# V units 0 to 119 of a two-block kernel: the weights stand in TensorE, 224 tokens move, and the result is transposed once

## The reference, cut to what matters

```python
def peer_ffn(xn, w_peer_q, sub_keys, expert_u, expert_v):
    ...                       # 128 experts and gates per token, expert_idx and gates
    def step(args):
        xc, ic, gc = args
        u = expert_u[ic]
        hval = jnp.einsum('cd,chkd->chk', xc, u).astype(jnp.float32)
        a = (gc * jax.nn.gelu(hval, approximate=False)).astype(xc.dtype)
        return jnp.einsum('chk,chkd->cd', a, expert_v[ic])
    ...
h = h + peer_ffn(rms_norm_2(h, norm_ffn_g[l]), ...)
return rms_norm_2(h, norm_final_g)
```

## Time and profile before

| | |
|---|---|
| median of 3 executions | 1364.8 us (1364.66 to 1365.86) |
| profiled execution | 1366.88 us, of which the trace spans 1365.1 us |
| PE busy | 1349.6 us (99% of the span) |
| PEld, DVE, ACT, POOL busy | 1169.7, 1060.6, 818.7, 161.5 us |
| U units 104 to 127 on TensorE | about 940.5 to 1003.9 us |
| V units 0 to 127 on TensorE | 1003.9 to about 1359.2 us |
| HBM traffic over the span | 200 GB/s read |

### The profile page before, as it was taken

The page is one execution under the profiler, slowest core; times in us unless marked ns, Lnnn a source line. Parts: engine busy times, 40 slices in busy tenths (PEclk is TensorE's granted clock), DMA queues, the critical chain, the costliest instruction groups (busy, mean ns, idle before and its releaser), DMA issues.

```text
span 1365.1 us, 21297 instructions
## 1 busy us (share of the span) xinstructions
PE 1349.6 (99%) x7896; PEld 1169.7 (86%) x7896; DVE 1060.6 (78%) x1965; ACT 818.7 (60%) x1568; POOL 161.5 (12%) x128
## 2 busy tenths in 40 slices
PE   8999999999999999999999999999999999999998
PEld 6998888888898888789999999999877777777776
DVE  6878676666787567679999899998887777777775
ACT  6876555555665554555556988886554444544444
POOL 3002030000000000000001100001333332333200
PEclk9999999999999999999999999999999999999999
DMA  6533466566544446655655544445889877777763
GB/s 223 185 120 116 136 221 187 189 194 189 167 159 137 141 139 228 203 169 172 214 188 189 193 157 153 157 156 184 298 285 348 291 286 267 280 291 287 274 197 100
DMA packets 77372, 275.38 MB, mean 202 GB/s; under 512 B 9845, under 2 KB 10357, under 8 KB 76886
## 3 DMA queue, kind: packets, MB, share of 16 engines
q1 hardware_dynamic: 67462, 239.52, 53.0%
q0 software_dynamic: 9808, 34.51, 6.6%
HBM read 270.94 MB, written 2.10 MB: 200 GB/s over the span
## 4 chain that ended last, share of the span: by engine, by line
PE 91%; DVE 4%; ACT 2%; issue 1%; DMA 1%; POOL 0%; SPq 0%; POOLq 0%; ACTq 0%; DVEq 0%
PE bank L2335 89%; DVE wl L624 1%; PE bank L2433 1%; DMA raw<-in_wts 1%; PE bank L2421 1%; ACT wh L1688 1%; DVE rows L1562 0%; ACT kdz L1694 0%; DVE St L814 0%; DVE x L1123 0%; DVE sgt L1121 0%; DVE t L774 0%; DVE us L1553 0%; DVE sg L768 0%; DVE St L811 0%
## 5 line engine op out<-in xcount | busy, mean ns | idle before, releaser
L624 DVE TENSOR_TENSOR wl<-raw,wh 128x1024 fp32r<-128x1024 f32 x429 | 523.0, 1226 | 178.3 <-ACT wh L1688 174.0
L1688 ACT ACTIVATE wh<-raw 128x1024 fp32r<-128x1024 f32 x429 | 449.1, 1055 | 240.8 <-PE bank L2335 232.4
L2335 PE MATMUL bank<-hTb,wh 128*128 128x224 f32 (+4 forms) x2208 | 560.8, 332 | 1.8 <-DVE wl L624 1.8
L2335 PE MATMUL bank<-wh,hTb 128*128 128x512 f32 (+1 forms) x1496 | 431.1, 395 | 2.2 <-DVE hTb L658 1.5
L2335 PE MATMUL bank<-hTb,wl 128*128 128x224 f32 (+2 forms) x1640 | 426.7, 274 | 0.0
L2335 PEld LDWEIGHTS bank<-hTb,wh 128*128 128x128 f32 (+1 forms) x2208 | 372.2, 190 | 26.7 <-ACT ga L2217 1.8
L2335 PEld LDWEIGHTS bank<-wh,hTb 128*128 128x128 f32 (+1 forms) x1496 | 267.5, 180 | 78.3 <-DVE hTb L1605 2.5
L2335 PEld LDWEIGHTS bank<-hTb,wl 128*128 128x128 f32 (+1 forms) x1640 | 312.1, 190 | 6.1
L2335 PE MATMUL bank<-wl,hTb 128*128 128x512 f32 (+1 forms) x748 | 247.6, 392 | 0.0
L2335 PEld LDWEIGHTS bank<-wl,hTb 128*128 128x128 f32 (+1 forms) x748 | 134.4, 180 | 36.2
L601 POOL DMA_INDIRECT rows<-in_u_rows,expert x32 | 55.9, 1745 | 299.0 <-DVE dots L1562 295.3
(11 more groups left out here) (410 smaller groups left out, 1382.9 us busy)
## 6 DMA issues: line engine op xcount, KB each, us to landing
raw<-in_wts SPq DMA_DIRECT2D x441, 512.0 KB, 3.5
x<-in_x SPq DMA_DIRECT2D x4, 256.0 KB, 7.4
sk<-in_sk SPq DMA_DIRECT2D x1, 1024.0 KB, 7.1
spill<-x SPq DMA_DIRECT2D x1, 1024.0 KB, 7.4
x<-spill SPq DMA_DIRECT2D x1, 1024.0 KB, 6.4
gb<-in_g_ffn SPq DMA_DIRECT2D x1, 512.0 KB
gb<-in_norm_mix_g SPq DMA_DIRECT2D x1, 512.0 KB
gb<-in_norm_ffn_g SPq DMA_DIRECT2D x1, 512.0 KB, 4.2
```

The source lines that it names most:

```text
L624: e.tensor_tensor(b[:, :], raw[u % RAW][:, :], a[:, :].bitcast(F), ALU.subtract).then_inc(S("lo"), 1)
L1688: e.activation(parts_of(u)[0][:, :], raw[u % RAW][:, :], ACT.Copy).then_inc(S("hi"), 1)
L2335: return e.matmul(o, l, r, start=first, stop=last, skip_group_check=True)
```

## The change

V units 0 to 119 (`DENSE = NE - 8`) are computed as the U units are: pieces of 128 columns of V rows stand in the array, and the tokens move, 448 columns (high and low) with `wh` and 224 with `wl`, 16 matmuls a unit (`part_V`). Piece k sums up over all 120 units in its own bank (`BANK_OF`), so all eight banks are in use. Units 120 to 127 are computed as before, into banks 0 to 3.

- At the start banks 2 to 5 still hold the last U units, so units 0 and 1 first go over the pieces in banks 0, 1, 6 and 7, then TensorE waits for the last U sum and goes over the other four. The last two U units' sums move from the V loop to where those of the others are.
- At the end of the 120 units the last four (`HOLD = 4`) go over the pieces in banks 0 to 3 (`FIRST`), then over those in 6, 7, 4 and 5 (`SECOND`). While the second half runs, ACT copies the low halves of the first four banks out (`lows_out`) and DVE adds the high halves (`evacuated`), and then unit 120 starts in these banks. The same follows for `SECOND` at n = 120.
- The eight sums have columns of V rows on partitions. After unit 121 TensorE turns them with 16 transposes into banks 4 to 7, and DVE adds these to `x` at n = 123 and 124 (`add_turned`).
- In the V loops `high_of` and `low_of` now come ahead of `high` and `low`. The additions of the gathered tokens (`folded`) come two units earlier, and TensorE waits before the last column range until bank 4 is free.

```diff
@@ -24,6 +24,8 @@
 SUMMED = NP + 1
 GATED = NP + 1 + NC
 SLOTS = 32
+HOLD = 4
+DENSE = NE - 8
 ORDER = list(range(NE - NP, NE)) + list(range(NE - NP - 1, -1, -1))
 K4 = (0, 1, 2, 3)
 SC = float(192) ** -0.5
@@ -127,8 +129,8 @@
         mhalf = sb("mhalf", [128, 16])
         warm = sb("warm", [128, 1])
         X0 = at[0]
-        ah = [sb(f"ah{i}", [128, 256], FR) for i in range(2)]
-        al = [sb(f"al{i}", [128, 256], FR) for i in range(2)]
+        ab = [sb(f"ab{i}", [128, 2, 256], FR) for i in range(2)]
+        ah, al = [t[:, 0, :] for t in ab], [t[:, 1, :] for t in ab]
         ge = [sb(f"ge{i}", [128, 256]) for i in range(2)]
         R0 = at[0]
         RE = nc.sbuf_usable_end // 32 * 32
@@ -390,6 +392,14 @@
                 return ah[n][:, 0:TN], al[n][:, 0:TN]
             return hTh[:, (n - 2) % 8, 0:TN], hTl[:, (n - 2) % 8, 0:TN]
 
+        def both_of(n):
+
+            return ab[n][:, :, 0:TN] if n < 2 else hTb[:, :, (n - 2) % 8, 0:TN]
+
+        def sums_of(k):
+
+            return gates[:, ORDER[k], :]
+
         def rows_of(q):
 
             return (128, TN - 128)[q]
...
+
+        BANK_OF = (0, 1, 6, 7, 2, 3, 4, 5)
+        FIRST, SECOND = (0, 1, 4, 5), (2, 3, 6, 7)
 
         ENDS = (slice(0, 512), slice(512, 768), slice(768, 1024))
         CUT = 448
@@ -1605,30 +1618,54 @@
                 e.tensor_tensor(b, gates[:, ORDER[n], :], a.bitcast(F), ALU.subtract).then_inc(S("al"), 1)
 
             at_u, at_v = slots_taken()
-            for n in range(GATED, NE - 2):
-                summed(n)
-                low(nth("U", ORDER[n]) + 2)
+            for n in range(GATED, NE):
+                if n < NE - 1:
+                    summed(n)
+                    low(nth("U", ORDER[n]) + 2)
+                else:
+                    low(nth("U", ORDER[n]) + 2)
+                    summed(n)
                 gated(n)
                 if n in (NE - 6, NE - 5):
                     low_of(n - NE + 6)
                 if n in at_u:
                     slot_taken(at_u.index(n))
+
+            def evacuated(ks, n):
+
+                for k in ks:
+                    e.wait_ge(S("u_out"), nth_sum("U", NE + n))
+                    e.tensor_tensor(sums_of(k), B[BANK_OF[k]][:, 0:TN], sums_of(k), ALU.add).then_inc(S("u_sum"), 1)
+                    n += 1
+
+            def add_turned(q):
+
+                e.wait_ge(S("in_end"), 48)
+                e.wait_ge(S("half"), 9 + q)
+                for n in range(2):
+                    xs = x[0:rows_of(q), q, two(512, n)]
+                    e.tensor_tensor(xs, B[4 + 2 * q + n][0:rows_of(q), :], xs, ALU.add).then_inc(S("used"), 1)
+
             for n in range(NE):
-                low(nth("D", "peer_expert_v_2", ORDER[n]) + LOOK)
                 if n + 2 < NE:
                     low_of(n + 2)
-                if n in (1, 2):
-                    summed(NE - 3 + n)
-                    gated(NE - 3 + n)
+                if n == DENSE - HOLD + 1:
+                    evacuated(FIRST, 0)
+                low(nth("D", "peer_expert_v_2", ORDER[n]) + LOOK)
                 if n in at_v:
                     slot_taken(at_v[n])
-                elif n - 6 in (max(at_v), max(at_v) + 1, max(at_v) + 2):
-                    folded(n - 6 - max(at_v))
+                elif n - 4 in (max(at_v), max(at_v) + 1, max(at_v) + 2):
+                    folded(n - 4 - max(at_v))
+                if n == DENSE:
+                    evacuated(SECOND, 4)
+                elif n in (DENSE + 3, DENSE + 4):
+                    add_turned(n - DENSE - 3)
             e.wait_ge(S("in_end"), 48)
+            e.wait_ge(S("used"), used_by(2 * SLOTS + 7))
 
             def add_end(n):
 
-                e.wait_ge(S("half"), 9 + n)
+                e.wait_ge(S("half"), 12 + n)
                 c, b = ENDS[n], end_of(ENDS[n])
                 if n == 1:
 
@@ -1638,11 +1675,11 @@
 
             def weighted_end(n):
                 c = ENDS[n]
-                e.wait_ge(S("used"), used_by(2 * SLOTS + 3))
+                e.wait_ge(S("used"), used_by(2 * SLOTS + 7))
                 e.wait_ge(S("x"), 19 + n)
                 e.tensor_tensor(h6[:, 1, c], x[:, 1, c], gb6[:, c], ALU.mult).then_inc(S("xg"), 1)
 
-            add_x(len(units) - 1, 8, 0)
+            add_x(len(units) - 1, 11, 0)
 
             def weighted(n):
                 c = two(512, n)
@@ -2296,21 +2333,30 @@
                     e.wait_ge(S("done"), nth("D", "peer_expert_v_2", ORDER[n - 8]) + 1)
                 copy(of_expert(n)[0], gates[:, ORDER[n], :]).then_inc(S("ah"), 1)
 
-            for n in range(GATED, NE - 2):
+            for n in range(GATED, NE):
                 block_out(n)
                 gelu(n)
                 if n in (NE - 6, NE - 5):
                     high_of(n - NE + 6)
+
+            def lows_out(ks):
+
+                for k in ks:
+                    copy(sums_of(k), B[BANK_OF[k]][:, TN:2 * TN]).then_inc(S("u_out"), 1)
+
             for n in range(NE):
-                high(nth("D", "peer_expert_v_2", ORDER[n]) + LOOK)
                 if n + 2 < NE:
                     high_of(n + 2)
-                if n in (1, 2):
-                    block_out(NE - 3 + n)
-                    gelu(NE - 3 + n)
+                if n == DENSE - HOLD + 1:
+                    e.wait_ge(S("half"), 8)
+                    lows_out(FIRST)
+                high(nth("D", "peer_expert_v_2", ORDER[n]) + LOOK)
                 if n == after_dots:
                     e.wait_ge(S("used"), used_by(SLOTS - 1))
                     e.activation(factor[:, :], dots[:, :], ACT.Gelu).then_inc(S("used"), 1)
+                if n == DENSE:
+                    e.wait_ge(S("done"), nth("D", "peer_expert_v_2", ORDER[DENSE - 1]) + 1)
+                    lows_out(SECOND)
             half_squares(5, 0, sq6)
 
             def scaled(q, c, made):
@@ -3082,13 +3128,49 @@
                 p.then_inc(S("G_ps"), 1)
             for n in range(GATED, NE):
                 early(n)
-            for n in range(NE - LAST):
-                if n == 0:
-                    e.wait_ge(S("G"), NC)
-                    e.wait_ge(S("gelu"), NE - 2)
+            def expert_of(n):
+
                 e.wait_ge(S("al"), FFT + n + 1)
-                unit_D(("D", "peer_expert_v_2", ORDER[n]), *of_expert(n), 0, n == 0, False,
+                return begin(("D", "peer_expert_v_2", ORDER[n]))
+
+            def part_V(held, n, ks):
+
+                both = both_of(n)
+                for k in ks:
+                    c, b = two(128, k), B[BANK_OF[k]]
+                    mm(b[:, 0:2 * TN], held[0][:, c], both, n == 0, False)
+                    t = mm(b[:, 0:TN], held[1][:, c], both[:, 0, :], False, n == DENSE - 1)
+                return t
+
+            e.wait_ge(S("G"), NC)
+            held = []
+            for n in range(2):
+                held.append(expert_of(n))
+                part_V(held[n], n, (0, 1, 2, 3))
+            e.wait_ge(S("u_sum"), nth_sum("U", NE - 1))
+            for n in range(2):
+                part_V(held[n], n, (4, 5, 6, 7)).then_inc(S("done"), 1)
+            for n in range(2, DENSE - HOLD):
+                part_V(expert_of(n), n, range(8)).then_inc(S("done"), 1)
+            held = []
+            for n in range(DENSE - HOLD, DENSE):
+                held.append(expert_of(n))
+                t = part_V(held[-1], n, FIRST)
+            t.then_inc(S("half"), 1)
+            for n in range(DENSE - HOLD, DENSE):
+                part_V(held[n - DENSE + HOLD], n, SECOND).then_inc(S("done"), 1)
+            e.wait_ge(S("u_sum"), nth_sum("U", NE + 3))
+            for n in range(DENSE, NE - LAST):
+                e.wait_ge(S("al"), FFT + n + 1)
+                unit_D(("D", "peer_expert_v_2", ORDER[n]), *of_expert(n), 0, n == DENSE, False,
                        tokens=(rows_of(0), rows_of(1)))
+                if n == DENSE + 1:
+                    e.wait_ge(S("u_sum"), nth_sum("U", NE + 7))
+                    for q in range(2):
+                        for k in range(8):
+                            p = e.transpose(B[4 + 2 * q + k // 4][0:rows_of(q), two(128, k % 4)],
+                                            sums_of(k)[:, 128 * q:128 * q + rows_of(q)], ident[:, :])
+                        p.then_inc(S("half"), 1)
 
             held = []
             for n in range(NE - LAST, NE):
@@ -3097,6 +3179,8 @@
                 t = part_D(held[-1], *of_expert(n), 0, 0, False, n == NE - 1)
             t.then_inc(S("half"), 1)
             for c in ENDS:
+                if c == ENDS[2]:
+                    e.wait_ge(S("used"), used_by(2 * SLOTS + 7))
                 for n in range(NE - LAST, NE):
                     (xh, xl), (wh_, wl_) = of_expert(n), held[n - NE + LAST]
                     for a, b, f in ((xh, wh_, c == ENDS[2] and n == NE - LAST), (xh, wl_, False), (xl, wh_, False)):
```

## The result

The changed kernel takes 1334.39 us (median of four executions, 1333.83 to 1336.55), the kernel before 1365.15 us beside it; ratio 0.9777, 95% interval 0.9760 to 0.9794. A second measurement of the same kernel gave 0.9782 (0.9768 to 0.9795).

A forecast was written before the change was run, and what follows sets the result against it. The prediction took TensorE's own pace in the V units as the bound. Pace saving 29.2 us minus 3.3 us for transposes, with joins and feed at nothing, gave 25.9 us less than 1364.8: 1338.9 us, range 1336.5 to 1346.

The forecast's parts named there:

- What bounds the kernel: V units: TensorE's own pace is the limit, busy for 99% of the span, with the feed waiting for it.
- Rival C: Feed becomes the limit in 107 V units sharing it with gathers, 0.125 us lost each, 1352 us; chance 0.09.
- Rival E: V units keep 2.76 us and only the transposes are added, 1368.1 us; chance 0.02.
- Rival D: Array loads in new V units no longer hidden, about 1418 us, or 1409 by the skill's rule; chance 0.03.
- The pace of the new units: V units 0 to 119: 2.760 us becomes 2.517, read from U units; 0.243 us saved each, 29.2 us in all.
- The query unit: A `w_peer_q_2` unit, 16 matmuls, 6144 columns, 2.83 us: second reading, giving 0.408 ns a column and 17 ns a matmul.
- The transposes: Between units 121 and 122: 16 transposes wholly on TensorE's path, 3.3 us more, bounds 3.0 and 3.5.
- The start: First V units, wait for the last U sum and new order: 1.5 us better to 3 us worse, taken as none.
- The joins: Start and end of the new V units: waits just covered, taken as 0; 1 to 3 us at the end if not.
- Both covers: First halves hide the waits: 2.5 us against 2.0 to 2.4 at the start; unit 120 covered by 0.9 us.
- rival B: One or more waits at start or end not covered, costing 2 to 6 us, about 1343 us; chance 0.12.
- The sum: Whole kernel: 29.2 us saved less 3.3 us added, 25.9 us less in all, giving 1338.9 us.

## Why the prediction was right or wrong

**What bounds the kernel: right.** TensorE's own pace did, and does after the change. Rival C (the feed) did not occur as a loss in every unit: in the changed kernel TensorE lost nothing in 107 units beside slots, though the loads' landings grew from 3.4 to 5.7 us. It isn't far off: in one of nine traces of the new form late loads cost 0.55 us near V unit 20. The prediction's reason, that `high` starts one unit earlier here than in the U units, fits; it wasn't tried by itself. Rival E did not occur either.

**Rival D and its rule: wrong, as the rows said.** With 16 loads of 128 columns a unit and the bank changing at every piece, the pace is 2.507 us. The rule that a load overlaps matmuls in flight only in other row groups (the Trainium skill, TensorE: Matmul & The Clock Gate, "The mechanism") would, taken by itself, have made the change a loss; this trace, with 2.507 us a unit, does not agree with it. The same section also names a background weight buffer as a case in which a load is pulled ahead of matmuls in flight, and that the prediction left out.

**The pace of the new units: 0.253 us saved, not 0.243.** The failed step is the reading of 2.517 us from U units as if they were the new units' twins. They end in a turned order (in the last piece the low part goes ahead of the high part), which costs 0.007 us a unit, and a V unit does not. The other 0.003 us is the place of the reading: an undisturbed U unit takes 2.513 us in the trace of before, and one of the three that were read took 2.520. Together 0.010 x 120 = 1.2 us too little gain. The query unit was no check of this: its 2.83 us drops out of 0.313 - 0.07, which is 2.760 - 2.517, and it ends in the turned order too. A check that doesn't share the reading is an estimate from the two paces of V units alone, both at a granted clock of 1.00: columns at 2.4 GHz and 17 ns for each matmul with its load give 12 x 17 + 2560 = 2764 ns (2760 measured) and 16 x 17 + 2240 = 2512 ns (2507 measured). The range's bound of 2.50 a unit did cover this term.

**The transposes: 1.67 us, not 3.3.** This is the failed step that cost most: the count behind the earlier trace rows. I took the eight records as four transposes, two records each, because a float32 product of the one-hot matmuls (`oi`, `oj`) does show two records. Transposes show one: 16 in the code are 16 records. So the earlier trace rows showed eight transposes in 0.80 us, and my bounds of 3.0 to 3.5 us excluded the true value. The trace of before could have told it: the 16 transposes of `x` have 16 records in all. The term was too large by 1.6 us, the biggest part of the miss.

**The start: 1.35 us gained, not nothing.** The prediction saw the old loss of 1.5 us, saw that the new order changes just that, gave -1.5 to +3 us as bounds and took 0. On the kernel before, the order alone brings 1.35 us: 1.03 by taking out the two late sums, and 0.32 at the last units, which the prediction hadn't seen. The failed step is putting this term at nothing between two bounds, although the operations that made the wait, the two late sums, were known to leave.

**The joins: right.** Both covers held, rival B did not occur. Without them TensorE waits 1.3 us at the start and 1.5 us at the end in the traces, so they are worth it, though the medians can't tell.

**The sum.** 25.9 + 1.2 + 1.6 + 1.35 = 30.05 us. The V stretch went from 354.51 to 324.66 us, 29.85 us less. The medians differ by 30.8 us; the 0.9 us more than the V stretch is within the ratio's interval, which spans 28.1 to 32.8 us. The three errors all lay on one side. The range's lower end was also too near by the prediction's own bounds: 0.017 x 120 = 2.0 us for the pace, 0.3 for the transposes and 1.5 for the start add up to 3.8 us, not to the 2.4 us that it allowed. Even 3.8 us would have given 1335.1, above the measured 1334.39, because the bounds of the transposes rested on the wrong count.

## What to carry to other kernels

Price a new loop by the same instruction mix in the trace, but compare also the order at the loop's edges, and check it against a sum by columns and matmuls from two other loops; a second reading that drops out of the result is no check. Before a price per instruction is taken from a merged row, find out how many records one instruction leaves, from a place where the code says how many were issued. And when an edit moves the very work that made a measured wait, the wait is a term of the sum, not a bound. Where a part that is due soon stands in a queue behind one that waits for a load, a late landing delays both; the other order cost nothing here.

## What was not expected of the hardware

A float32 transpose of 128 x 128 has a duration of 0.27 us in the records, but in a row they start 0.109 us apart, and 16 of them with the start of the next matmul take 1.67 us.

Eight pairs of a 448- and a 224-column matmul take 7 ns longer when the last pair is turned round, so that two long ones and two short ones follow each other, with the same operands and columns.

With units a tenth faster and 302 in place of 283 GB/s (both from 1060 to 1290 us), the median landing of a 512 KB load went from 3.4 to 5.7 us while the DMA share rose only from 0.79 to 0.87.
